# Attention by pairs of heads, with convolution matmuls between the parts of a pair, in a one-layer encoder block

## What is computed

```python
h = rms_norm(x, norm_mix)                       # x: 1024 tokens x 1024, f32
x_in, b_g, c_g, q, k, v, gate_a, gate_b = split(h @ w_in)
y_conv = (b_g * conv3(c_g * x_in)) @ w_out_conv             # 512 channels
q, k = rms_norm per head (8 heads x 64)
y_attn = neighbourhood_attention(q, k, v, rpb) @ w_out_attn
x = x + (sigmoid(gate_a) * y_conv + sigmoid(gate_b) * y_attn) @ w_o
x = x + moe_ffn(rms_norm(x, norm_ffn))          # 32 experts, top 4
```

## Time and profile before

| | us |
|---|---|
| median of 3 runs | 2500.72 (2492.02 to 2501.24) |
| profiled execution, own time | 2496.67 |
| its span | 2494.9 |
| projection of q, k, v | 0 to 190.4 |
| attention and convolution | 190.4 to 533.0 |
| merge | 533.0 to 826.1 |
| output projection, routing, experts | 826.1 to the end |

### The profile page before, as it was taken

The page is one execution under the profiler, slowest core; times in us unless marked ns, Lnnn a source line. Parts: engine busy times, 40 slices in busy tenths (PEclk is TensorE's granted clock), DMA queues, the critical chain, the costliest instruction groups (busy, mean ns, idle before and its releaser), DMA issues.

```text
span 2494.9 us, 34927 instructions
## 1 busy us (share of the span) xinstructions
PE 2375.1 (95%) x11110; PEld 1516.1 (61%) x11111; DVE 1461.0 (59%) x1906; ACT 1043.5 (42%) x1068; POOL 932.2 (37%) x512
## 2 busy tenths in 40 slices
PE   8997999999999995899999999999999999999996
PEld 4443444456666553677766666666666666666774
DVE  3301333341111245688877787777778787777885
ACT  2111222231101002476655565565565565565663
POOL 3210111100000002667664465446357365455663
PEclk9998999999999997899999999999999999999998
DMA  4114110101111323699987888888889888789994
GB/s 153 68 42 110 34 42 25 34 9 51 50 27 59 110 102 146 241 352 337 340 294 264 283 287 287 309 282 296 294 298 317 295 289 291 270 299 298 327 337 153
DMA packets 180117, 505.34 MB, mean 203 GB/s; under 512 B 18082, under 2 KB 60578, under 8 KB 180066
## 3 DMA queue, kind: packets, MB, share of 16 engines
q1 hardware_dynamic: 163874, 457.97, 51.6%
q0 software_dynamic: 16192, 46.67, 8.4%
HBM read 468.34 MB, written 32.05 MB: 201 GB/s over the span
## 4 chain that ended last, share of the span: by engine, by line
PE 85%; DVE 7%; issue 4%; DVEq 1%; ACT 1%; SPq 1%; DMA 1%; POOL 0%; ACTq 0%; POOLq 0%; PEldq 0%
PE psum L1465 14%; PE psum L1467 12%; PE psum L1466 12%; PE psum L1253 7%; PE psum L1310 7%; PE psum L1411 5%; PE psum L1346 4%; PE psum L1476 4%; DVE w_lo L1076 3%; PE psum L1357 2%; PE psum L1356 2%; PE psum L1358 2%; PE psum L1511 2%; PE psum L1294 2%; PE psum L1273 2%
## 5 line engine op out<-in xcount | busy, mean ns | idle before, releaser
L1076 DVE TENSOR_TENSOR w_lo<-ring,w_hi 128x2048 fp32r<-128x2048 f32 x384 | 874.0, 2305 | 70.9 <-ACT w_hi L734 54.4
L734 ACT ACTIVATE w_hi<-ring 128x2048 fp32r<-128x2048 f32 x384 | 721.9, 1919 | 164.4 <-DMA ring<-in_w_down 93.2
L574 POOL TENSOR_SCALAR pick<-iota_bf,slot_col 128x256 bf16<-128x256 bf16 x264 | 526.5, 2007 | 62.5 <-DVE slot_col L1089 62.4
L1465 PE MATMUL psum<-w_hi,xT_hi 128*128 128x512 f32 x1024 | 424.1, 414 | 42.6 <-DVE w_lo L1076 30.2
L1467 PE MATMUL psum<-w_hi,xT_lo 128*128 128x512 f32 x1024 | 407.0, 397 | 0.0
L1466 PE MATMUL psum<-w_lo,xT_hi 128*128 128x512 f32 x1024 | 406.5, 397 | 0.0
L1465 PEld LDWEIGHTS psum<-w_hi,xT_hi 128*128 128x128 f32 x1024 | 193.5, 189 | 164.4 <-issue 71.8
L580 POOL DMA_INDIRECT xg<-h_rows,idx_new x33 | 83.5, 2530 | 548.5 <-issue 519.1
L1467 PEld LDWEIGHTS psum<-w_hi,xT_lo 128*128 128x128 f32 x1024 | 193.6, 189 | 46.9
L1466 PEld LDWEIGHTS psum<-w_lo,xT_hi 128*128 128x128 f32 x1024 | 194.3, 190 | 39.8
L1465 PE MATMUL psum<-w_hi,aT_hi 128*128 128x512 f32 x512 | 215.0, 420 | 3.3 <-DVE aT_lo L1113 3.3
(11 more groups left out here) (247 smaller groups left out, 3094.7 us busy)
## 6 DMA issues: line engine op xcount, KB each, us to landing
ring<-in_w_gate SPq DMA_DIRECT2D x256, 512.0 KB, 5.3
ring<-in_w_up SPq DMA_DIRECT2D x256, 512.0 KB, 6.6
ring<-in_w_down SPq DMA_DIRECT2D x256, 512.0 KB, 5.8
ring<-in_w_in SPq DMA_DIRECT2D x28, 512.0 KB, 4.7
ring<-in_x SPq DMA_DIRECT2D x16, 512.0 KB, 4.1
ring<-in_w_in SPq DMA_DIRECT2D x6, 1024.0 KB, 7.2
vb<-oT SPq DMA_DIRECT2D x16, 256.0 KB, 6.6
ring<-in_w_o SPq DMA_DIRECT2D x4, 1024.0 KB, 6.0
```

The lines of the kernel that those rows point to most:

```text
L574: e.tensor_scalar(pick[:, t, :], iota_bf[:, :], slot_col[:, t, :], None, ALU.is_equal).then_inc(g_pick, 1)
L734: e.activation(w_hi[:, hs, :], ring[:, slot, :], ACT.Copy).then_inc(g_hi, 1)
L1076: e.tensor_tensor(w_lo[:, hs, :], ring[:, slot, :], w_hi[:, hs, :].bitcast(F32), ALU.subtract).then_inc(g_lo, 1)
L1465: e.matmul(dst, hi, w_up, start=start, stop=False)
```

## The change

Its edits, one by one:

- The columns are projected in the order v, k, q. On SP the 16 moves into `vb` now stand ahead of items 6 to 9, and items 4 and 5 behind the bias stores. The stores of zeros read a cleared part of `qkT`, not of `oT`.
- Attention goes by pairs: heads 2hp and 2hp + 1 of one query block, 32 pairs. `scores` issues the even head on partitions 0 to 63 and the odd one on 64 to 127, into banks 2 and 3. `weighted` alternates the two heads, with outputs on partitions 0 to 63 and 64 to 127 of one bank.
- Within a pair n TensorE has `scores(n)`, three matmuls of the convolution, `weighted(n - 1)`, two or three further matmuls, `prob_transpose(n)` with six transposes. `conv_at[n]` counts single matmuls; twelve come before pair 0.
- One ScalarE copy takes both heads' transposed probabilities, one VectorE copy both heads' results. There are two `prob` buffers and one double `probT`.
- VectorE does the taps one at a time (`one_tap`), behind `mins` and behind the rest of a pair.
- Pool loads two heads' windows at once and holds three bias variants of two heads. It computes all x scales first.
- `w_used` is gone. Who loads a slot waits for the work that reads it (`wait_read`).
- In the first merge tile the `ypre` part stands ahead of the last `weighted`. The first output tile starts at `mixd` = 15.

```diff
-        prob = [rb_[:, 384 * i:384 * i + 384] for i in range(3)]
-        probT = [rb_[:, 1152 + 384 * i:1152 + 384 * i + 384] for i in range(2)]
+        prob = [rb_[:, 384 * i:384 * i + 384] for i in range(2)]
+        probT = rb_[:, 768:1536].rearrange("p (h n) -> p h n", h=2)
...
-        for c0 in (2048, 1536, 2560):
+        for c0 in (2560, 2048, 1536):
...
+        pairs = HEADS // 2 * 8
+        CSTEPS = 24 * KT
+        conv_at = [12 + (CSTEPS - 12) * n // pairs for n in range(pairs + 1)]
...
             def scores(n):
+                hp, rb, cb, v = pair(n)
+                if n == 0:
                     e.wait_ge(qev, q_evacs(2 * TT))
                 else:
+                    e.wait_ge(smin, 2 * n)
                 q0 = 512 * rb + P * cb
+                for i in range(2):
+                    kg = qkT[HD * i:HD * i + HD, hp, :].rearrange("p (r c) -> p r c", c=GRID_W)
+                    e.matmul(bank[2 + i][:, 0:KEYS].rearrange("p (r c) -> p r c", c=KC), qkT[HD * i:HD * i + HD, 4 + hp, q0:q0 + P],
+                             kg[:, ROW_BASE[rb]:ROW_BASE[rb] + KR, COL_BASE[cb]:COL_BASE[cb] + KC], start=True, stop=True).then_inc(sc, 1)
...
+                for t in range(3):
+                    for i in range(2):
+                        ins = e.matmul(bank[6 + n % 2][HD * i:HD * i + HD, 0:P], vb[:, cb, rb + t, HD * (2 * hp + i):HD * (2 * hp + i) + HD],
+                                       probT[:, i, P * t:P * t + P], start=(t == 0), stop=(t == 2))
                 ins.then_inc(pvd, 1)
...
+            conv_steps(0, KT)
+            q_transpose(2 * TT - 1)
+            conv_steps(KT, conv_at[0])
+            for n in range(pairs):
+                scores(n)
+                conv_steps(conv_at[n], conv_at[n] + 3)
+                if n:
+                    weighted(n - 1)
+                conv_steps(conv_at[n] + 3, conv_at[n + 1])
+                prob_transpose(n)
...
+            conv_products(0, conv_at[0] // KT)
+            for n in range(pairs):
+                mins(n)
+                conv_products(conv_at[n] // KT, (conv_at[n] + 3) // KT)
+                one_tap(taps_ready(conv_at[n] + 3))
+                normalise(n)
+                if n:
+                    attn_out(n - 1)
+                conv_products((conv_at[n] + 3) // KT, conv_at[n + 1] // KT)
+                one_tap(taps_ready(conv_at[n + 1]))
+            attn_out(pairs - 1)
...
+            conv_values(0, conv_at[0] // KT)
+            for n in range(pairs):
+                if n:
+                    probs_out(n - 1)
+                conv_values(conv_at[n] // KT, (conv_at[n] + 3) // KT)
+                exps(n)
+                conv_values((conv_at[n] + 3) // KT, conv_at[n + 1] // KT)
+            probs_out(pairs - 1)
...
+                    if n == 0 and g == 1:
+                        weighted(pairs - 1)
+                        e.wait_ge(oev, pairs)
...
-                if t == 0:
-                    e.wait_ge(mixd, 16)
-                if t >= 2:
+                if t < 2:
+                    e.wait_ge(mixd, 15 + t)
+                else:
                     e.wait_ge(e_x1, 2 * (t - 1))
```

More of the change, by code:

```diff
@@ L338, in wait_item, with wait_read, pair @@
             e.wait_ge(w_in[n % MSLOT], landed[n])
-        NCONST = 7
[L342 to L346, removed]
+        def wait_read(e, n):
+            if n < IT_CONV:
+                e.wait_ge(proj, TT * (n // 2 + 1))
+            elif n < IT_MERGE:
+                e.wait_ge(proj, 3 * TT + 6 * ((n - IT_CONV) // 2) + (4, 6)[(n - IT_CONV) % 2])
+            else:
+                e.wait_ge(mtile, 8 * ((n - IT_MERGE) // 2) + 8)
+        NCONST = 7
+        pairs = HEADS // 2 * 8
+        CSTEPS = 24 * KT
+        conv_at = [12 + (CSTEPS - 12) * n // pairs for n in range(pairs + 1)]
+        def pair(n):
+            hp, b = n // 8, n % 8
             rb, cb = b // 4, b % 4
-            return h, rb, cb, 3 * rb + COL_VAR[cb]
+            return hp, rb, cb, 3 * rb + COL_VAR[cb]
         def q_evacs(n):
@@ L650, in transposed @@
                         ins.then_inc(qev, 1)
+            for t in range(TT):
+                if t + 2 < TT:
+                    x_squares(t + 2)
+                e.wait_ge(proj, t + 1)
+                e.activation(vnat[:, t, :], bank[t % 2][:, :], ACT.Copy).then_inc(vev, 1)
             for n in range(2 * TT):
-                if n + 2 < TT:
-                    x_squares(n + 2)
                 squares(n)
@@ L657, in _ @@
                     transposed(n - 1)
[L658 to L665 removed]
+            transposed(2 * TT - 1)
             def exps(n):
[L669 to L671 removed]
+                for i in range(2):
+                    e.wait_ge(smin, 2 * n + i + 1)
+                    e.activation(prob[i], prob[i], ACT.Exp, bias=nmin[:, i:i + 1], scale=-1.0, accum_out=rsum[:, i:i + 1]).then_inc(sexp, 1)
@@ L673, in probs_out @@
             def probs_out(n):
                 e.wait_ge(ptr, n + 1)
[L675 to L690, removed]
@@ L691, in _, with conv_values @@
-            probs_out(units - 2)
-            probs_out(units - 1)
+                if n:
+                    e.wait_ge(pvd, n)
+                e.activation(probT, psum[:, 4 * 512:6 * 512].rearrange("p (h n) -> p h n", h=2)[:, :, 0:KEYS], ACT.Copy).then_inc(pev, 1)
+            def conv_values(m0, m1):
+                for m in range(m0, m1):
+                    j, part, hf = m // 6, (m % 6) // 2, m % 2
+                    if part == 0:
+                        e.wait_ge(proj, 3 * TT + m + 1)
+                        if j >= 2:
+                            e.wait_ge(cconv, j - 1)
+                        e.activation(u[j % 2][:, 512 * hf:512 * hf + 512], bank[m % 2][:, :], ACT.Copy).then_inc(uev, 1)
@@ L700, in _ @@
             round_gate_weights(0)
-            e.wait_ge(oev, units)
+            e.wait_ge(oev, pairs)
             for k in range(KT):
```

248 lines of the change are left out of this document (114 added, 134 removed).

## The result

The changed kernel takes 2399.39 us (median of 4 runs, 2398.68 to 2400.60), the kernel before, beside it, 2500.93: a ratio of 0.9601, 95% interval 0.9589 to 0.9614, so 101.5 us less.

What follows compares the result with a forecast made beforehand. TensorE, busy 95% of the span, was taken as the bound; 85.9 less in attention and merge start, plus 0.4, 2.2 and 1.0, minus 2.5 kept back, gave 87 less: forecast 2414 us, range 2403 to 2438.

Steps and rivals of the forecast that it cites:

- The stretch: Attention, from the projection's last block to the merge: 342.6 us before, TensorE's sum 250.8 after.
- the tail: End of attention: last `weighted` 0.80, copy to `oT` and wake-up 0.5 us; 4.7 us with the merge's convolution products ahead.
- late first bias and taps: Attention: first minimum up to 2.3 us late, at most 0.5 seen; taps meeting two pairs; 1.5 us allowed.
- Full overlap: Pairs in attention: two heads' scores take 0.84 us and weighted sums 0.80, the low ends of the bounds.
- the rivals: Attention: row halves do not overlap, 20.5 us more, chance 0.09; neither kind overlaps, 20.5 + 21.1 more, chance 0.04.
- the ordered halves: Rival in attention pairs: matmul halves start in program order, 14 us more, 2428; chance 0.05.
- The softmax chain: Attention pairs: products end near 4.4 us, slack 1.9 or more; the rival that it sets the pair, 2446, chance 0.04.
- The experts see nothing but an earlier start: Behind the output projection: the experts would only start earlier, with no gain of their own.
- 2.2 us in the merge: Merge: TensorE's waits for its own completion go, seven of 0.3 us, 2.2 us gained.
- the output projection: It may start 2.1 us earlier, but two weight loads start late: 1 us taken, bounds 0 and 3.8.
- the 2.5 us kept back for clock falls: Whole sum: 2.5 us of the 89.5 held back for one clock fall or two that may survive.
- it lies 4 us under the median: Whole kernel: the profiled execution lies 4 us under the median 2500.7, so about 2410 became a forecast of 2414.

Runs made afterwards that it cites:

- e4: Kernel before with only the values projected first and their moves into `vb` early, units of one head as before: 2482.66 us.
- e5: e4 with the three taps spread over the three units behind the product, still units of one head: 2463.48 us.
- e1: Changed kernel with both score matmuls of a pair on the same half of the rows, using the even head: 2436.46 us, merge starts 20.0 us later.
- e2: Changed kernel with both heads' weighted sums on the same 64 output rows, one head after the other: 2454.71 us, merge starts 20.3 us later.
- e3: Changed kernel with the even head's three weighted-sum matmuls ahead of the odd head's, still on two column halves: 2408.54 us, merge starts 9.3 us later.
- e7: Changed kernel with the convolution's matmuls in whole groups of eight again, so ten of 32 pairs have none between their parts: 2428.63 us.
- e9: Changed kernel with 83 always satisfied waits added on TensorE in the program's first steps: 2401.59 us.
- e12: Changed kernel run again without any change, beside the same runs of the kernel before: 2399.41 us.
- e6: Changed kernel with the three taps in one burst again: 2401.23 us.
- e8: Changed kernel with TensorE's waits for its own completion back in the merge and the output projection starting at `mixd` = 16: 2403.01 us.
- e10: Changed kernel with all of a pair's convolution steps between scores and transposes, then the previous pair's weighted sums: 2393.78 us.

## Why the prediction missed its range

The kernels of the chain, by medians: before 2500.9, values first 2482.7, taps spread 2463.5, pairs with single steps and the rest 2399.4.

**The stretch: right.** Predicted 86.3 us up to the second merge tile (85.9, and 0.4 from the projection), measured 88.3. The sum for the stretch was 250.8; from the first convolution matmul (189.44) to the merge (440.42) it is 251.0. That it fits so well is partly luck: the sum counts all 32 weighted sums, and the tail counts the last one, 0.80, again, while in the run it stands in the merge; and a pair took 6.99 or 7.85 us where the sum has 6.97 and 7.82, which is 0.8 over 32 pairs. Of the 2.0 over, 0.6 are the projection, which gave 1.0 (its stretch ends at 189.44, not 190.43), and 1.5 were stalls allowed for late first bias and taps: the first minimum started at once, at 201.22, behind a window load of 5.1 to 6.8 us where I took 9, and no tap was seen. The values were worth 18 us by the medians of e4 (15.3 by the profiled executions) and the burst with its clock 19 by e5, as the two steps had them.

**Full overlap: right, for row halves too.** This was an inference from four column strips. e1 and e2 price the two divisions at 20.0 and 20.3 us, where the rivals had 20.5 and 21.1. Neither rival, nor the ordered halves, came. The Trainium skill ("TensorE: Matmul & The Clock Gate", section "Part 3: Packing small matmuls — row/col tiling") has matmuls start and finish in program order. Two heads that start 7 ns apart agree with it as long as whole matmuls are counted; counted by halves, as the prediction did, they do not, since the odd head's first half then passes the even head's second. The head-by-head run does not agree either way: its second chain starts at 0.275 us, ahead of the first chain's last matmul at 0.487. By the rule counted in halves e3 would have cost 17.5 us; it cost 9.3.

**The softmax chain: right.** 4.4 us predicted, 3.9 measured, and no wait. e7 shows the cover gone: 21.4 us of waits.

**Failed: what lies behind the stretch.** The step "The experts see nothing but an earlier start" is the one that fell. Routing gave 2.3 us and the experts 2.4. The first is the entry to the loop: the branch there took 3.45 us before and 0.37 after, and e9's waits alone bring 3.36 back. The second goes with the kernels' instructions, not with their work, which is 11110 matmuls in each. Between the remainder matmuls of the same two experts lie 1004.9 to 1005.0 us in the three kernels with the old attention (before, e4, e5) and 1003.5 to 1003.8 in the changed one, e3 and e7 to e12, with 1004.2 in e6. From the last remainder matmuls to the end it is 224.4 to 225.0 us in the first three and 223.0 to 223.6 in the others. e9's waits don't bring these back. What does is open.

**Mis-sized: "2.2 us in the merge".** It gave 3.9. e8 puts 2.3 on those waits; the rest, 1.5, goes with something else that differs there, perhaps the counting of `w_used`; I had counted only what the list of waits names.

**Mis-sized: the output projection.** 1 us was taken; up to its last matmul it gave 1.4. My reason for the bound was right (the weights wait, e8), and my reason for the gain was not: e8 starts late and still takes 132.4 us. What its window lacks is the clock fall of the kernel before (1.00 against 0.90). As e8 has the wait and no fall, it isn't shown that the change took the fall away; it may have been luck.

**Mis-sized: the 2.5 us kept back for clock falls.** Once the clock has risen, at 13 us, there are none until 869 us. This was caution without a row behind it.

**The profile's own offset.** Added up against the spans: 2.5 kept back, 2.0 in the stretch, 1.7 merge, 0.4 output projection, 2.3 routing, 2.4 experts, so 11.3 of 98.3. The other 3.3 of the 14.6 us between 2414 and 2399.4 is the step "it lies 4 us under the median": the distance of profiled run and median belonged to the kernel before, whose runs differ by their clock falls. Without falls the changed kernel's profiled run lies 0.7 under its median, not 4. The falls are removed by the change, so their scatter should have been, too. With 98.3 + 3.3 the 101.5 is closed to 0.1. Every one of these terms errs to the same side, and the range's low end had no room for that.

## What to carry to other kernels

Two small matmuls on different halves of the array, of rows or columns, cost what one costs, if they are issued alternately: look for the pair (heads, blocks) that can share the array, and then count the changes between divided and whole, 0.19 us each here: the order of e10, with one less in a pair, was the faster. Spread an independent chain's single steps, not its groups, into the places where another engine's chain must be hidden; once the slack and the engine's own idle time nearly cover a burst, other smoothing is worth little. When a change removes waits behind which the clock fell, compare spans to spans, and expect the scatter of the runs to go with them.

## What the runs showed of the hardware

- Halves for two row halves start 7 ns apart. Head by head, TensorE passes over about three waiting halves (the second chain starts at 0.275 us).
- A branch of TensorE's took 3.45 or 0.37 us by what stood ahead of it in the program; 83 satisfied waits, 41 instructions, moved the following matmul by 3.0 us (40.95 against 37.95). In the dear cases a 16 KB block of instructions arrives during the branch.
- The granted clock falls to the lower level for 3.4 or 6.8 us shortly after TensorE has waited some 2 us: behind all four such waits in the stretch of the kernel before and of e4, behind four of ten (1.8 to 2.9 us) in e7, not behind the 2.2 us of e8, and never in the stretch of e5 and the changed kernel, which don't wait so long.
